# The up projection of a two-layer decoder with stationary tokens, in pairs of column blocks and partly by Strassen's seven products

## The reference

```python
x = x + merged @ w_out[l]
h2 = rms_norm(x, norm2_g[l])
x = x + jnp.square(jax.nn.relu(h2 @ w_up[l])) @ w_down[l]
```

## Time and profile before

| | us |
|---|---|
| median of 3 runs | 2854.45 (2853.38 to 2855.43) |
| the profiled execution | 2853.83 |
| its span, first to last instruction | 2852.0 |
| TensorE busy in it | 2837.5 |

### The profile page before, as it was taken

The page is one execution under the profiler, slowest core; times in us unless marked ns, Lnnn a source line. Parts: engine busy times, 40 slices in busy tenths (PEclk is TensorE's granted clock), DMA queues, the critical chain, the costliest instruction groups (busy, mean ns, idle before and its releaser), DMA issues.

```text
span 2852.0 us, 34495 instructions
## 1 busy us (share of the span) xinstructions
PE 2837.5 (99%) x13800; PEld 2376.9 (83%) x13800; DVE 1913.5 (67%) x2072; ACT 1467.2 (51%) x1937; POOL 182.6 (6%) x205
## 2 busy tenths in 40 slices
PE   8999999999999999999999999999999999999999
PEld 7888888888888888888888888888888888888887
DVE  6788655555677686776556976556556776867754
ACT  5777644444544444444448776444444444444443
POOL 1125100000000000000001250000000000000000
PEclk9999999999999999999999999999999999999999
DMA  8655566756656566575566555566566565665654
GB/s 299 209 170 172 168 195 204 239 189 206 179 191 199 170 221 183 186 233 183 187 220 215 160 174 173 197 206 236 192 199 185 177 209 165 223 185 177 213 186 147
DMA packets 340320, 557.86 MB, mean 196 GB/s; under 512 B 13216, under 2 KB 144288, under 8 KB 337984
## 3 DMA queue, kind: packets, MB, share of 16 engines
q1 hardware_dynamic: 334416, 526.68, 56.3%
q0 software_dynamic: 5744, 28.97, 3.3%
HBM read 549.32 MB, written 6.29 MB: 195 GB/s over the span
## 4 chain that ended last, share of the span: by engine, by line
PE 98%; DMA 1%; ACT 0%; DVE 0%; issue 0%; SPq 0%; DVEq 0%
PE acc L656 17%; PE acc L658 17%; PE acc L657 17%; PE acc L672 17%; PE acc L673 9%; PE acc L879 5%; PE acc L880 5%; PE acc L881 5%; PE tp L685 2%; DMA raw<-in_w_in 1%; PE tp L879 0%; PE tp L880 0%; PE sc L880 0%; PE sc L879 0%; PE tp L881 0%; PE sc L881 0%
## 5 line engine op out<-in xcount | busy, mean ns | idle before, releaser
L1346 DVE TENSOR_TENSOR lo<-raw,hi 128x1024 fp32r<-128x1024 f32 (+1 forms) x816 | 1001.7, 1230 | 787.5 <-ACT hi L1010 780.6
L1010 ACT ACTIVATE hi<-raw 128x1024 fp32r<-128x1024 f32 (+1 forms) x816 | 852.2, 1046 | 1086.0 <-PE acc L658 651.6
L672 PE MATMUL acc<-hT,hi 128*128 128x512 f32 x2048 | 724.2, 399 | 0.0
L673 PE MATMUL acc<-hT,lo 128*128 128x256 f32 x2048 | 575.2, 281 | 0.0
L656 PE MATMUL acc<-hi,hT 128*128 128x512 f32 x1280 | 509.8, 398 | 5.6 <-DVE lo L1346 5.6
L658 PE MATMUL acc<-hi,hT 128*128 128x512 f32 x1280 | 499.8, 390 | 0.0
L657 PE MATMUL acc<-lo,hT 128*128 128x512 f32 x1280 | 498.6, 390 | 0.0
L672 PEld LDWEIGHTS acc<-hT,hi 128*128 128x128 f32 x2048 | 384.8, 188 | 95.9
L673 PEld LDWEIGHTS acc<-hT,lo 128*128 128x128 f32 x2048 | 386.9, 189 | 0.3
L656 PEld LDWEIGHTS acc<-hi,hT 128*128 128x128 f32 x1280 | 240.5, 188 | 54.9 <-issue 3.7
L1252 ACT ACTIVATE hi<-raw 128x1024 fp32r<-128x1024 f32 x168 | 174.0, 1056 | 215.8 <-PE acc L881 112.0
(11 more groups left out here) (296 smaller groups left out, 2908.4 us busy)
## 6 DMA issues: line engine op xcount, KB each, us to landing
raw<-in_w_in SPq DMA_DIRECT2D x159, 1024.0 KB, 5.0
raw<-in_w_up SPq DMA_DIRECT2D x128, 1024.0 KB, 5.5
raw<-in_w_down SPq DMA_DIRECT2D x128, 1024.0 KB, 5.1
raw<-in_w_out SPq DMA_DIRECT2D x32, 1024.0 KB, 5.1
raw<-in_w_mem_kv SPq DMA_DIRECT2D x16, 1024.0 KB, 5.1
raw<-in_w_attn_o SPq DMA_DIRECT2D x16, 1024.0 KB, 5.1
raw<-in_w_conv_o SPq DMA_DIRECT2D x8, 1024.0 KB, 5.0
raw<-in_w_mem_o SPq DMA_DIRECT2D x8, 1024.0 KB, 5.1
```

What stands on the lines that cost most here:

```text
L672: pe.matmul(acc[:, pair, j, :], w1, hT[:, :, kt, :], start=first, stop=last, skip_group_check=True)
L673: mm = pe.matmul(acc[:, pair, j, 0:SEQ], w2, hT_hi[:, kt], start=False, stop=last, skip_group_check=True)
L1010: act.activation(hi[:, u % 4, :, 0:w], raw[:, c, 2 * (u % 2):2 * (u % 2) + 2, 0:w], ACT.Copy).then_inc(hi_ready, 1)
L1346: dve.tensor_tensor(lo[:, u % 4, :, 0:w], raw[:, here.ring[u // 2], 2 * (u % 2):2 * (u % 2) + 2, 0:w], hi[:, u % 4, :, 0:w].bitcast(F32), ...
```

## The change

The up projection gets the form of the down projection: stationary tokens (`hT`), moving weights, two column blocks at a time by `seven_products`, with u = 0, 1 of each block by seven products. A quarter then has four pairs, j = 0, 1 of the up projection and j = 2, 3 of the down projection. The hidden state now leaves TensorE with tokens in rows, in PSUM and partly in `u_sum`; it is added up in `u_sum` (DVE), squared (ACT), transposed by eight fills a quarter and taken to `bT_hi` and `bT_lo` in the pair that follows. The sums of tokens for the up projection are made once a layer. The down projection of the last quarter of the second layer is in pairs now as well; that of the first layer stays plain. The chunks of `w_up` have 512 columns and 4 rows a partition in place of 256 and 8. The parking of `x_tok` moves behind the 17th unit of a layer, and POOL's first loads of the second layer wait for the last pair of the first. At the end, the last unit finishes one block of token rows ahead of the other, and the last block's output goes out in two halves.

```diff
+PARK_AT = 17
...
+def pair_number(l, qu, j):
+
+    return PAIRS_BEFORE[l] + PAIRS_A_QUARTER * qu + j
...
+def paired(l, qu):
+
+    return qu < FFN // D - 1 or l == LAYERS - 1
...
-                    cols = slice((b0 + b) * COL, (b0 + b + 1) * COL)
-                    sp.dma_start(raw[:, slots[k]], v_down[l, qu, c, :, :, cols]).then_inc(landed[slots[k]], 16)
+                    sp.dma_start(raw[:, slots[k]], source[c, :, :, bass.ds(c0 + b * COL, COL)]).then_inc(landed[slots[k]], 16)
...
+                    for j in range(2):
+                        load_pair(pair_number(l, qu, j), v_up[l], qu * D + 2 * j * COL)
+                    if paired(l, qu):
+                        for j in range(2):
+                            load_pair(pair_number(l, qu, 2 + j), v_down[l, qu], 2 * j * COL)
                         continue
...
+                for t in range(T) if b == CB - 1 else (None,):
+                    rows_ = slice(0, T) if t is None else slice(t, t + 1)
+                    sp.wait_ge(x_new, LAYERS * (CB + CB * FFN // D) - CB + b + 1 + (t or 0))
+                    sp.dma_start(out_tokens.rearrange("t p d -> p t d")[:, rows_, cols], x_tok[:, rows_, cols]
+                                 ).then_inc(out_done, 16)
...
-            def up_unit(s, u, pair):
-
-                if u == 0:
...
-                        pe.matmul(acc[:, pair, j, :], w1, hT[:, :, kt, :], start=first, stop=last, skip_group_check=True)
-                        mm = pe.matmul(acc[:, pair, j, 0:SEQ], w2, hT_hi[:, kt], start=False, stop=last,
-                                       skip_group_check=True)
...
+            def hidden_fill(i, qu, j):
+
+                if i in HID_FILL:
+                    k = HID_FILL.index(i)
+                    if k % 2 == 0:
+                        pe.wait_ge(hid_squared, here.next("hid"))
+                    fill(("hid", qu, j, k), [u_sum[:, HID_SLOT[k], n * P:(n + 1) * P] for n in range(4)])
...
+            def seven_products(l, qu, j):
+
+                pair = pair_number(l, qu, j)
+                first_of_layer = qu == j == 0
+                a_hi, a_lo = (hT_hi, hT_lo) if j < 2 else (bT_hi, bT_lo)
+                s_hi, s_lo = (hT_sum_hi, hT_sum_lo) if j < 2 else (hidT_sum_hi, hidT_sum_lo)
+                p1, p5, p6, p7 = sc_seen[:, 0], tp_seen[:, 0], tp_seen[:, 1], sc_seen[:, 1]
...
+                    if j == 2 and b == 0:
+                        hidden_here(u, qu)
...
                     if u < SEVEN and b == 0:
                         product(p1, *a[0][0], *w[0], u == 0, u == SEVEN - 1)
                         mm = product(acc[:, 1, 0], *a[1][0], *w[1], u == 0, False)
                     elif u < SEVEN:
-                        mm = product(acc[:, 0, 0], sT_hi[:, 3, u], sT_lo[:, 3, u], *w[1], u == 0, False)
+                        mm = product(acc[:, 0, 0], s_hi[:, 3, u], s_lo[:, 3, u], *w[1], u == 0, False)
+                    elif pair == LAST_PAIR and i == 15:
+                        product(acc[:, 0, 0], *a[0][0], *w[0], False, False)
+                        product(acc[:, 0, 0], *a[1][0], *w[1], False, True).then_inc(rows_summed, 1)
+                        product(acc[:, 0, 1], *a[0][1], *w[0], False, False)
+                        mm = product(acc[:, 0, 1], *a[1][1], *w[1], False, True)
                     else:
                         for dk in range(2):
                             end = u == UNITS - 1 and dk == 1
                             product(acc[:, 1 - b, 0], *a[dk][0], *w[dk], False, end)
                             mm = product(acc[:, 1 - b, 1], *a[dk][1], *w[dk], u == SEVEN and dk == 0, end and b == 1)
...
+                    if j in (1, 2):
+                        hidden_fill(i, qu, j - 1)
...
+            def hidden_here(u, qu):
+
+                if u == 0:
+                    emptied(*(("hid", qu, 0, k) for k in range(4)))
+                if u == 4:
+                    emptied(("hid", qu, 1, 0), ("hid", qu, 1, 1))
+                if u == 6:
+                    emptied(("hid", qu, 1, 2), ("hid", qu, 1, 3))
+
+            def mlp(last, qu, l):
+
+                for j in range(4):
+                    if j < 2 or paired(l, qu):
+                        seven_products(l, qu, j)
                         continue
...
+            def hidden_of_pair(i, l, qu, j, with_sums):
+
+                done = 2 * (2 * (l * (FFN // D) + qu) + j)
+                for k, n in enumerate(HID_FILL):
+                    if i == n + EMPTY_AFTER:
+                        kts, cols = slice(8 * j + 4 * (k // 2), 8 * j + 4 * (k // 2) + 4), slice(k % 2 * P, (k % 2 + 1) * P)
+                        take_high(("hid", qu, j, k), bT_hi[:, kts, cols],
+                                  whole=tokens[:, :, cols] if with_sums and k < 2 else None)
+                for b, n in enumerate(HID_SQUARED_AT):
+                    if i == n:
+                        block = u_sum[:, b::2]
+                        act.wait_ge(hid_summed, done + b + 1)
+                        act.activation(block, block, ACT.Relu).then_inc(hid_above, 1)
+                        act.wait_ge(hid_above, done + b + 1)
+                        act.activation(block, block, ACT.Square).then_inc(hid_squared, 1)
...
+            def rest_of_up_pair(i, pair, qu, j, units):
+
+                if i == 0:
+                    dve.wait_ge(w_sum_used, pair + 1)
+                    dve.wait_ge(seven_free, pair + 1)
+                    step(add_to_u(0, acc[:, 1, 0]))
+                    step(add_to_u(2, acc[:, 1, 1]))
+                    settle()
+                    dve.sem_inc(acc_free[1], 1)
+                    dve.sem_inc(hid_summed, 1)
+                if i == 2:
+                    dve.wait_ge(unit_done, units + 4)
+                    step(add_to_u(3, acc[:, 0, 0]))
+                if i == 3:
+                    step(add_to_u(1, acc[:, 0, 1]))
+                    settle()
+                    dve.sem_inc(acc_free[0], 1)
+                    dve.sem_inc(hid_summed, 1)
+                for k, n in enumerate(HID_FILL):
+                    if i == n + EMPTY_AFTER:
+                        kts, cols = slice(8 * j + 4 * (k // 2), 8 * j + 4 * (k // 2) + 4), slice(k % 2 * P, (k % 2 + 1) * P)
+                        here.next("fill")
+                        take_low(("hid", qu, j, k), bT_lo[:, kts, cols], bT_hi[:, kts, cols])
...
+            def last_rest():
+
+                b0 = CB - 2
+                dve.wait_ge(seven_free, LAST_PAIR + 1)
+                settle()
+                step(add_to_x(0, b0, u_sum[:, 0]))
+                step(add_to_x(1, b0, acc[:, 1, 1]))
+                step(add_to_x(0, b0 + 1, u_sum[:, 3]))
+                step(add_to_x(1, b0 + 1, u_sum[:, 1]))
+                settle()
+                add_to_x(1, b0, u_sum[:, 2]).then_inc(x_new, 1)
+                dve.wait_ge(rows_summed, 1)
+                add_to_x(0, b0 + 1, acc[:, 0, 0]).then_inc(x_new, 1)
+                dve.wait_ge(unit_done, here.now("unit") + 4)
+                add_to_x(1, b0 + 1, acc[:, 0, 1]).then_inc(x_new, 1)
...
+                        if with_sums and i == TOKEN_SUMS_AT:
+                            token_sums(SUMS_BEFORE[l] + 2 + qu)
+                        side_of_pair(i, pair, slots, units, None if j < 2 else 2 * (j - 2))
+                        if with_sums and i == TOKEN_SUMS_AT + 3:
+                            sums_low(SUMS_BEFORE[l] + 2 + qu, hidT_sum_lo, hidT_sum_hi)
+                    else:
+                        split(m % UNITS, COL)
+                    if j in (1, 2):
+                        rest_of_up_pair(i, pair - 1, qu, j - 1, units)
+                    if j == 3 and paired(l, qu):
+                        rest_of_pair(i, pair - 1, 0, units)
+                    if j == 0 and qu > 0:
+                        rest_of_pair(i, pair - 1, 2, units)
...
+                    pool.wait_ge(unit_done, l * GROUPS * UNITS + 4 + PARK_AT)
+                    alone()
+                    for t in range(T):
+                        pool.dma_start(x_park[t], x_tok[:, t]).then_inc(parked, 16)
...
-                for t in range(T):
-                    pool.dma_start(x_park[t], x_tok[:, t]).then_inc(parked, 16)
```

277 lines of the change are left out of this document (119 added, 158 removed).

## The result

| | before | after |
|---|---|---|
| median | 2854.11 us (4 runs) | 2828.74 us (2828.23 to 2829.36, 4 runs) |
| ratio to before | | 0.991 (95%: 0.9897 to 0.9923) |
| span of the profiled execution | 2852.0 | 2827.0 |
| TensorE's granted clock | full | full |

The changed kernel is faster by 25.4 us. The prediction was 2823.5 us, and its range, 2819 to 2834, holds the result.

The account below looks back on a forecast made before the run. TensorE was taken as the bound, busy 2837.5 of 2852.0 us at full clock. Terms -48.7 + 23.0 - 2.7 - 3.2 - 0.9 + 1.6 = -30.9 us gave 2823.5 us, range 2819 to 2834.

Parts of the forecast that it names:

- form and seven products: Eight up projections, each 372 matmuls at the down pairs' pace, 84.35 us in place of 90.44: 48.7 us less.
- fills: 64 groups of four transposes of the hidden state among TensorE's matmuls, 0.36 us each, not hidden: 23.0 us more.
- last down quarter, 12 matmuls: Second layer's last down projection: 384 matmuls become 372, 2.7 us less.
- parking: First layer: moving the 2 MB store of x_tok later removes TensorE's waits for lo, 3.2 us less; bounds 0 and 3.7.
- end: After the last matmul: one DVE instruction instead of two, 0.7 us less, and half the output bytes, 0.2 less.
- waits behind ACT and DVE: TensorE waits 0.15 us in seven j = 1 pairs and 0.5 in the plain down quarter: 1.6 us more.
- the three brackets: TensorE's three first-layer waits for lo, at 55.11, 59.10 and 62.53: 1.81 + 0.98 + 0.39 = 3.2 us, all taken as saved.
- the rival by which the old pace was not the form's: Up projections: new matmuls go no faster there, because of what runs beside them; near 2849 us, chance 0.02.
- The count of the pair j = 1: Up pair with token sums: DVE finishes unit 10's lo at 22.0 us, TensorE arrives at 21.9, waiting 0.1 to 0.2.
- The rival of a longer chain: ACT and DVE work in up pairs takes 0.4 to 1.5 us a pair more than counted; 2829 to 2847, chance 0.14.
- Late weights: Up pairs: TensorE waits if weights take above 7.2 us to land; 2862 us at 9.6, chance 0.04.
- Full rows of the fills: Transposes in up and down pairs cost their full rows, 0.27 us each: 47 us more, near 2871, chance 0.01.

Follow-up runs that it names:

- eight products: Changed kernel with one of the seven products of sums made three times in each of 16 up pairs: 2850.96 us, 22.2 more.
- the late load: Changed kernel with the sixth weight chunk of every pair asked for one unit later: 2845.33 us, 16.6 more.
- the run with one transpose: Changed kernel with one transpose in place of four in every fill of the hidden state: 2819.07 us, 9.7 less.

## Why the prediction was right, and where it was off

Measured against predicted, in us:

| term | predicted | measured | from |
|---|---|---|---|
| form and seven products | -48.7 | -48.7 | the new matmuls' 226.8 ns; eight products +22.2 |
| fills | +23.0 | +29.4 | 16 stages x (86.19 - 84.35) |
| last down quarter, 12 matmuls | -2.7 | -2.7 | -0.88 = 1.84 - 2.72 |
| parking | -3.2 | -2.85 in the profile | -4.2 behind the front's first matmul, +1.4 ahead of it; 2.1 to 4.1 by the medians |
| end | -0.9 | -1.0 | 4.96 - 3.93 |
| waits behind ACT and DVE | +1.6 | +0.8 | the rest |
| sum | -30.9 | -25.1 | span: -25.0 |

**The mis-sized term** is *Fills*: "a fill among matmuls costs the distance of the starts around it less one matmul: 0.36 us". The mechanism held, four transposes are overlapped and not hidden, but a fill costs 0.46 us. The distance around it is as predicted; the missing 0.1 lies in the matmuls behind. A transpose costs 0.108 us, but the matmul behind the last one starts 0.03 us after it, and the rest shows one matmul later. It stood in the rows of before too: the matmul behind the one at 395.27 starts 0.32 us later.

```profile
395.59 0.39 PE L657 MATMUL acc<-lo,hT 128*128 128x512 f32 x1
```

64 x 0.10 = 6.4 us, where the sum of the terms was 5.9 us off (-30.9 against -25.0); the other terms miss by 0.5 together. A whole stage would have come nearer: the first up projection of a layer, with eight transposes more than the others, took 91.32 against 90.44, 0.44 for four.

That the parking's term is near is in part luck: with the late parking this part of the front lost 4.1 us, more than the 3.2 of the three brackets, and the later first matmul of the profiled execution, with which the parking has nothing to do, took 1.4 of it back.

**Form and pace.** The new matmuls go at 226.8 ns with `hT` as with `bT_hi`, so the rival by which the old pace was not the form's is refuted. But "the form with tokens stationary is quicker" says too much: kept at 512 columns, the old form goes at 226.7 ns as well. It was slower for having two matmuls where the new has one and a half, and for mixing two lengths. The Trainium skill ("TensorE: Matmul & The Clock Gate", Back-to-back issue gap) gives N / 2.4 + 2.5 ns for an isolated matmul, an estimate of 215.8 and 109.2 ns for 512 and 256 columns; the runs show 226.8 and 120.3, which is 11 ns more for either length, and go before it.

**ACT and DVE.** The count of the pair j = 1 had `lo` of unit 10 ready 22.0 us behind the pair's start, and 963.11 - 941.07 = 22.04 was measured. It had TensorE there at 21.9, and TensorE came at 963.34 - 941.07 = 22.27, because its four fills took 1.84 us and not 1.4. So no wait shows: the mis-sized fill turned a wait of 0.1 us into a slack of 0.2, and that this unit is the tight one held. Of the 0.8 us, 0.27 are in the plain down quarter behind the last up pair (0.5 was taken), 0.45 in the first up projections (87.30 where 86.19 + 0.88 would be 87.07), where the first of the eight transposes of the norm starts 0.36 us behind its matmul in place of 0.23, and the rest are the hundredths by which the others exceed 86.19. The rival of a longer chain didn't come, but was near: two fills placed one unit later cost 5.7 us, one DVE instruction 8.7.

**Late weights.** `w_up` does land later, 6.0 against 5.5 us, and this hides in the spare 2.0 us of unit 10, as the late load shows. **Full rows of the fills** are refuted: 0.46 us for four, not 1.1. **The end** gave what was counted, one DVE row of 0.75 behind the last matmul in place of 1.41:

```profile
2823.07 0.39 PE L879 MATMUL acc<-hi,bT_lo 128*128 128x512 f32 x1
2823.49 0.75 DVE L1687 SCALAR_TENSOR_TENSOR x_tok<-acc,squared_rstd,x_tok 128x512 f32<-128x512 f32 x1 [0.61 <-PE acc L879]
```

**Open.** The scatter of the front has three parts in the profiles: the first matmul at 11.5 to 12.9 us, the half clock behind it in six of thirteen (1.4 to 1.6 us), and the load that the early parking makes late by more or less. Why the first matmul comes later, and why the same wait is followed once by the full and once by the half clock, was not traced, so the parking's worth is known only as 2 to 4 us. Pairing the plain down quarter of the first layer as well, 12 matmuls or 2.7 us by this count, was not tried.

## What to carry to other kernels

Where one engine is the bound, price an insertion over a whole stage that has it against one that lacks it: the distance around it misses what the next instructions lose (here 0.1 of 0.46 us, 64 times). Look for waits inside both stages first: read from stages with a wait, as in the run with one transpose, the price comes out wrong. For the same columns, prefer few matmuls of one length, whichever operand is stationary. And when work is moved under a bound engine, count the chain of the other engines unit by unit to its last consumer: their busy share (73% here) said nothing of a place that had 0.23 us left.

## What was not expected of the hardware

- A matmul with its own weight load cost its columns at 2.4 GHz (0.416 ns each) and 13.5 ns, for 256 and for 512 columns; a weight load whose row lasts 188 ns did not hold back matmuls 120.3 ns apart.
- Matmuls of 512 and 256 columns by turns cost 6.2 ns a couple more than the two apart.
- Among matmuls of 512 columns one transpose cost 0.14 us, four 0.46 and eight 0.90: 0.108 each and 0.03 for the break, with 0.1 us of it in the matmuls behind.
- Behind a wait of 2.2 us at 55.6 us, in a row of matmuls, the granted clock fell to 0.50 and matmuls of 512 columns went 0.427 us apart for some 3 us; before, with a wait of 1.8 us at the same place, kept 1.00. At the front's first matmul a wait of 2.3 to 2.4 us was followed by the half clock in six profiles and by the full one in six.
- `w_up` landed in 6.0 us where it took 5.5. It isn't the shape of its rows alone, if at all: `w_down`, whose chunks are as before, went from 5.1 to 5.5. The cause was not looked for.
